# The 64-byte phase of the weight slots that TensorE loads for 256 moving columns: (3, 0) in place of (1, 1)

## The chip, the cores and the metric

One core of one Trainium2 chip. The metric is the device time of one execution in microseconds (us); durations of single instructions are in nanoseconds (ns).

## The reference

Two transformer blocks run one after the other on 256 tokens of width 2048, in float32. The first mixes a state-space branch (SSD) and an attention over selected keys, the second is a softmax attention with forget gates ("Fox"). Each is followed by an MLP with a squared ReLU and 8192 hidden units. Cut to what is large:

```python
def hybrid_layer(x, ...):
    h = rmsnorm(x, g_mix) @ w_in                      # one wide input projection, split into parts
    ...                                               # convolution, SSD, attention
    x = x + concat([y_ssd, y_att]) @ w_out
    u = rmsnorm(x, g_mlp) @ w_up
    return x + square(relu(u)) @ w_down

def second_block(x, ...):
    h = fox_attention(rmsnorm(x, g0), w_in, b_f, w_out)
    x = x + rmsnorm(h, g1)
    h = square(relu(rmsnorm(x, g2) @ w1)) @ w2
    return x + rmsnorm(h, g3)
```

## The kernel before

Each float32 operand is split into a high part (rounded to the type fp32r) and a low part (the rest), and a product is made of three: high by high, high by low and low by high.

The weights stream through a ring of four slots. A slot holds 128 partitions x 2048 values (1024 KB in all). The queue of SyncE brings a chunk into `raw`; ScalarE (ACT) copies it to `wh`, which rounds it (L671); VectorE (DVE) writes raw minus wh to `wl` (L1208), and wl lies in the same memory as raw. TensorE (PE) uses the slot and adds one to `chunk_used`; that lets SyncE refill it. Four slots in a row make a panel of 512 output columns.

Where a slot lies is set by `slot`: its base is a multiple of 256 bytes, and a *phase* moves it by 0 to 3 steps of 64 bytes (`ASIDE` is 16 values of four bytes). Each panel has a pair of phases, one for wh (high) and one for raw and wl (low):

```python
high, low = PHASES.get((b, j), PHASES.get(b, (0, 0)))
at = j * SLOT + ASIDE * (high if buffer is wh else low)
```

The activations (`XHL`, with `XH` and `XL` in it) start on multiples of 256 bytes throughout.

PE takes the panels in four forms:

- *narrow* (`k_tile`, lines 2213 to 2215): the weights are the stationary operand, 128 x 128 at a time, and 256 columns of XH or XL move. For each of the 64 blocks of a panel there are three matmuls: wh by XH, wh by XL, wl by XH, each with a weight load of its own. Eight panels are narrow: the first five of the input projection (`WIN`), the first panel of each MLP (`B_M1`, `B_M2`) and the first of the Fox projection (`B_FOX`). A panel has four slots of 48 such matmuls. Their phases are (1, 1).
- *wide* (`half_cols`, lines 2200 and 2202): wh by 512 columns (XH and XL together), then wl by the 256 of XH. These are the other panels of the MLPs' first products, with phases (1, 0) in the first half of an MLP, behind a first slot ("lead") with (1, 3), and (3, 0) in the second half behind a lead with (3, 2); and seven panels of the Fox projection with (3, 0).
- *rows* (lines 2173 to 2175) and the MLPs' second products (lines 2319 to 2321): the weights are the moving operand, with phases (0, 0).

The order of all this on PE is written out by hand. Between slots PE also does side work by two tables (`MIX_AT`, `FOX_AT`), such as transposes and the small products of the attention. In the opening and at the start of the second MLP it turns pieces of the activations every few matmuls.

Of the kernel before, what the change touches and what calls it, by code (L numbers as in the profile page):

```python
# [73 lines left out]
def hybrid_then_fox(nc, x, g_mix, w_in, conv_w, conv_b, dt_bias, a_log, d_skip, g_ssd, g_q, g_k,  # L74
# [3 lines left out]
    with ctx:  # L78
# [232 lines left out]
        def fox_acc(n):  # L311
# [6 lines left out]
        narrow_chunks = ({B_WIN + n for n, (kind, _) in enumerate(WIN) if kind in TFORM}  # L318
                         | {B_FOX, B_M1, B_M2})
# [1 line left out]
                       | {b0 + half * B_HALF + n for b0 in (B_M1, B_M2) for half in range(2) for n in range(UP)}  # L321
                       - narrow_chunks)

        PHASES = {b: (1, 1) for b in narrow_chunks}
        PHASES.update((b, (3, 0)) for b in wide_chunks)
        for b0 in (B_M1, B_M2):
            for half in range(2):
                first = b0 + half * B_HALF + (half == 0)
                lead, rest = ((3, 2), (3, 0)) if half else ((1, 3), (1, 0))
                PHASES.update((b, rest) for b in wide_chunks if first <= b < first + UP)  # L330
                PHASES[first, 0] = lead

        def slot(buffer, b, j):


            high, low = PHASES.get((b, j), PHASES.get(b, (0, 0)))
            at = j * SLOT + ASIDE * (high if buffer is wh else low)
# [2343 lines left out]
```

How the kernel before makes its waits and increments, by code:

```python
        def wait_full(eng, name):  # L449
            b, n = uses[name]
            eng.wait_ge(side_full[b], n + 1)
# [1 line left out]
        def wait_emptied(eng, name):  # L453
            b, n = uses[name]
            eng.wait_ge(side_free[b], n + 1)
# [1 line left out]
        def wait_free(eng, name):  # L458
            b, n = uses[name]
            if n:
                eng.wait_ge(side_free[b], n)
# [1 line left out]
        def full(ins, name):  # L463
            ins.then_inc(side_full[uses[name][0]], 1)
# [18 lines left out]
            def chunk(w, b, j, k0, col):  # L483
                if not (isinstance(b, int) and b == 0):
                    sp.wait_ge(chunk_used, 4 * b + j - 3)
                src = w[k0 * P:(k0 + 4) * P, col].rearrange("(k p) n -> p k n", p=P)
                sp.dma_start(slot(raw, b, j), src).then_inc(raw_landed[j], 16)
# [5 lines left out]
            def half_panels(w, b, col, kept={}):  # L494
                for j in range(4):
                    sp.wait_ge(chunk_used, 4 * b + j - 3)
                    c, r = col + 256 * (j // 2), 8 * P * (j % 2)
                    sp.dma_start(slot(raw, b, j).rearrange("p a (c n) -> p (a c) n", n=256),
                                 w[r:r + 8 * P, c:c + 256].rearrange("(k p) n -> p k n", p=P))\
                      .then_inc(raw_landed[j], 16)
                    if j in kept:
                        at = (slice(0, P), kept[j] // 2, slice(1024 * (kept[j] % 2), 1024 * (kept[j] % 2) + 1024))
                        sp.wait_ge(sum_ready, 12)
                        sp.dma_start(kept_x[at], X[at]).then_inc(x_kept, 16)
```

## Time and profile before

| | us |
|---|---|
| median of 3 runs | 2182.21 (2181.88 to 2183.65) |
| span of the profiled execution | 2179.8 |
| PE busy | 2162.5 |
| DVE busy | 1437.6 |
| ACT busy | 1026.6 |

The page gives no time of the profiled execution other than its span, which runs from the first instruction to the last. PE's matmuls overlap: one starts while the one before it still drains, so the sum of their durations is larger than the busy time, and the distance between two starts tells how fast they go. In the rows below, PE is TensorE's matmuls, and the rows name an instruction by its line in the kernel and by output and inputs.

### The profile page before, as it was taken

To read this page: it belongs to the slowest core of one execution; us is meant where nothing else is said; L and a number is where in the kernel's file an instruction comes from. 1 tells how busy PE (TensorE), PEld (TensorE's weight loads), DVE (VectorE), ACT (ScalarE), POOL (GpSimd) and SP (SyncE) were. 2 spreads that over 40 slices of the span, in tenths; PEclk is the share of its full clock that TensorE was granted. 3 is DMA by queue.
4 is the path that set the end of the run, shared out by engine and by line. 5 is a ranking of instruction groups with operands and counts; after the bars stand their busy time and mean duration, and the time that the engine had idled before them with its cause. 6 is when DMAs were issued, how large, how long until landed. Compare 5 with 4: busy or idle time off the path is not lost.

```text
span 2179.8 us, 27888 instructions
## 1 busy us (share of the span) xinstructions
PE 2162.5 (99%) x11744; PEld 1867.4 (86%) x11744; DVE 1437.6 (66%) x1748; ACT 1026.6 (47%) x1176; POOL 26.3 (1%) x71
## 2 busy tenths in 40 slices
PE   9999999999999999999999999999999999999998
PEld 9988788988888888888898888889888888888886
DVE  6688664566666766687756654546666766667787
ACT  6453563444443444445444444545444444445453
POOL 1000000000000000000001010000000000000000
PEclk9999999999999999999999999999999999999999
DMA  8455445566666666666566665556666666666665
GB/s 263 144 171 166 153 135 193 174 193 194 193 195 196 203 195 194 193 196 200 186 196 203 189 190 172 174 193 196 206 193 193 197 194 200 194 194 192 204 217 188
DMA packets 256413, 415.49 MB, mean 191 GB/s; under 512 B 13284, under 2 KB 167056, under 8 KB 256032
## 3 DMA queue, kind: packets, MB, share of 16 engines
q1 hardware_dynamic: 254800, 409.89, 59.9%
q0 software_dynamic: 1456, 3.81, 0.6%
q8 instruction: 93, 1.52, 0.3%
q14 instruction: 32, 0.26, 0.0%
q10 hardware_dynamic: 32, 0.01, 0.0%
HBM read 409.47 MB, written 4.21 MB: 190 GB/s over the span
## 4 chain that ended last, share of the span: by engine, by line
PE 96%; DVE 3%; ACT 0%; issue 0%; POOL 0%; DVEq 0%; POOLq 0%; ACTq 0%
PE bank L2200 25%; PE bank L2202 12%; PE bank L2320 10%; PE bank L2321 10%; PE bank L2319 10%; PE bank L2173 5%; PE bank L2175 5%; PE bank L2174 5%; PE bank L2213 3%; PE bank L2215 3%; PE bank L2214 3%; DVE wl L1208 1%; PE bank L2436 1%; PE bank L2261 1%; PE bank L2457 0%; PE bank L2466 0%
## 5 line engine op out<-in xcount | busy, mean ns | idle before, releaser
L1208 DVE TENSOR_TENSOR wl<-raw,wh 128x2048 fp32r<-128x2048 f32 x376 | 860.1, 2290 | 355.0 <-ACT wh L671 353.7
L671 ACT ACTIVATE wh<-raw 128x2048 fp32r<-128x2048 f32 x376 | 721.0, 1919 | 466.4 <-DVE raw L1458 138.4
L2200 PE MATMUL bank<-XHL,wh 128*128 128x512 f32 x2368 | 810.1, 390 | 0.0
L2202 PE MATMUL bank<-XHL,wl 128*128 128x256 f32 x2368 | 654.2, 276 | 0.0
L2200 PEld LDWEIGHTS bank<-XHL,wh 128*128 128x128 f32 x2368 | 444.5, 188 | 93.3 <-issue 0.2
L2202 PEld LDWEIGHTS bank<-XHL,wl 128*128 128x128 f32 x2368 | 444.5, 188 | 0.3
L2319 PE MATMUL bank<-wh,hh 128*128 128x512 f32 x844 | 328.6, 389 | 0.0
L2320 PE MATMUL bank<-wl,hh 128*128 128x512 f32 x844 | 328.4, 389 | 0.0
L2321 PE MATMUL bank<-wh,hl 128*128 128x512 f32 x844 | 328.3, 389 | 0.0
L2173 PE MATMUL bank<-wh,XHL 128*128 128x512 f32 x576 | 229.4, 398 | 0.7 <-DVE XHL L1216 0.7
L2175 PE MATMUL bank<-wh,XHL 128*128 128x512 f32 x576 | 224.7, 390 | 0.0
L2174 PE MATMUL bank<-wl,XHL 128*128 128x512 f32 x576 | 224.2, 389 | 0.0
L797 ACT ACTIVATE RB<-bank 128x256 f32<-128x256 f32 x120 | 39.6, 382 | 345.4 <-PE bank L2202 345.4
L2319 PEld LDWEIGHTS bank<-wh,hh 128*128 128x128 f32 x844 | 158.4, 188 | 33.1
L2320 PEld LDWEIGHTS bank<-wl,hh 128*128 128x128 f32 x844 | 158.4, 188 | 32.9
L2321 PEld LDWEIGHTS bank<-wh,hl 128*128 128x128 f32 x844 | 158.4, 188 | 32.5
L1378 DVE TENSOR_TENSOR RB<-bank,RB 128x256 f32<-128x256 f32 x120 | 45.3, 419 | 198.2 <-ACT RB L797 198.2
L2213 PE MATMUL bank<-XHL,wh 128*128 128x256 f32 x512 | 145.7, 284 | 3.0 <-DVE XHL L1242 1.2
L2214 PE MATMUL bank<-XHL,wh 128*128 128x256 f32 x512 | 142.7, 279 | 0.0
L2215 PE MATMUL bank<-XHL,wl 128*128 128x256 f32 x512 | 142.7, 279 | 0.0
L2175 PEld LDWEIGHTS bank<-wh,XHL 128*128 128x128 f32 x576 | 108.1, 188 | 23.3
L2173 PEld LDWEIGHTS bank<-wh,XHL 128*128 128x128 f32 x576 | 108.2, 188 | 22.8 <-DVE XHL L1216 1.0
(445 smaller groups left out, 1832.7 us busy)
## 6 DMA issues: line engine op xcount, KB each, us to landing
raw<-in_mlp_w_dram SPq DMA_DIRECT2D x128, 1024.0 KB, 5.5
raw<-in_w_up_dram SPq DMA_DIRECT2D x64, 1024.0 KB, 5.4
raw<-in_w_down_dram SPq DMA_DIRECT2D x64, 1024.0 KB, 5.5
raw<-in_fox_w_in_dram SPq DMA_DIRECT2D x48, 1024.0 KB, 5.3
raw<-in_w_in_dram SPq DMA_DIRECT2D x40, 1024.0 KB, 5.0
raw<-in_w_out_dram SPq DMA_DIRECT2D x16, 1024.0 KB, 5.0
raw<-in_fox_w_out_dram SPq DMA_DIRECT2D x16, 1024.0 KB, 5.0
raw<-in_w_in_dram SPq DMA_DIRECT2D x16, 256.0 KB, 8.3
```

The source lines that it names most:

```text
L671: act.activation(slot(wh, b, j), slot(raw, b, j), ACT.Copy).then_inc(hi_ready, 1)
L1208: dve.tensor_tensor(slot(wl, b, j), slot(raw, b, j), slot(wh, b, j).bitcast(F32), ALU.subtract)\
L2173: pe.matmul(o, sh, mh, start=first and kk == 0, stop=False)
L2174: pe.matmul(o, sh, ml, start=False, stop=False)
L2175: mm = pe.matmul(o, sl, mh, start=False, stop=last and kk == 3)
L2200: pe.matmul(bk[:, :].rearrange("p (s t) -> p s t", s=2), sh, XHL[:, k, :, :], start=k == 0, stop=False, skip_group_check=True)
L2202: mm = pe.matmul(bk[:, 0:TOK], sl, XH[:, k, :], start=False, stop=k == KT - 1, skip_group_check=True)
L2213: pe.matmul(o, sh, mh, start=first and f % 2 == 0, stop=False, skip_group_check=True)
L2214: pe.matmul(o, sh, ml, start=False, stop=False, skip_group_check=True)
L2319: pe.matmul(bk[:, :], a[0], w[0], start=first, stop=False)
L2320: pe.matmul(bk[:, :], a[0], w[1], start=False, stop=False)
L2321: return pe.matmul(bk[:, :], a[1], w[0], start=False, stop=last)
```

## The change

The pair of phases of the eight narrow panels becomes (3, 0): wh lies 192 bytes beyond a multiple of 256 instead of 64, raw and wl lie on it instead of 64 beyond. All other panels keep theirs. No instruction is added or taken away.

```diff
-        PHASES = {b: (1, 1) for b in narrow_chunks}
+        PHASES = {b: (3, 0) for b in narrow_chunks}
         PHASES.update((b, (3, 0)) for b in wide_chunks)
         for b0 in (B_M1, B_M2):
             for half in range(2):
```

## Rows read from the trace of the kernel before

**Rows 1.** The page's head and its busy time of PE.
```profile
span 2179.8 us, 27888 instructions
...
PE 2162.5 (99%) x11744; PEld 1867.4 (86%) x11744; DVE 1437.6 (66%) x1748; ACT 1026.6 (47%) x1176; POOL 26.3 (1%) x71
```
**Rows 2.** The page's chain that ended last, by engine.
```profile
PE 96%; DVE 3%; ACT 0%; issue 0%; POOL 0%; DVEq 0%; POOLq 0%; ACTq 0%
```
**Rows 3.** The page's costliest groups: count, busy us, mean ns of one.
```profile
L1208 DVE TENSOR_TENSOR wl<-raw,wh 128x2048 fp32r<-128x2048 f32 x376 | 860.1, 2290 | 355.0 <-ACT wh L671 353.7
L671 ACT ACTIVATE wh<-raw 128x2048 fp32r<-128x2048 f32 x376 | 721.0, 1919 | 466.4 <-DVE raw L1458 138.4
...
L2213 PE MATMUL bank<-XHL,wh 128*128 128x256 f32 x512 | 145.7, 284 | 3.0 <-DVE XHL L1242 1.2
L2214 PE MATMUL bank<-XHL,wh 128*128 128x256 f32 x512 | 142.7, 279 | 0.0
```
**Rows 4.** Timeline of PE, second panel's first slot: start us, duration us.
```profile
33.52 0.28 PE L2213 MATMUL bank<-XHL,wh 128*128 128x256 f32 x1
...
39.18 0.26 PE L2517 MATMUL bank<-ident,PR 110*128 110x110 f32 x1
```
**Rows 5.** Timeline of PE, third panel's first slot.
```profile
61.70 0.28 PE L2213 MATMUL bank<-XHL,wh 128*128 128x256 f32 x1
...
67.15 0.33 PE L2507 MATMUL bank<-ident,SMT 96*128 96x96 f32 x2
```
**Rows 6.** Windows, L2214 alone: length, busy (count), granted clock, DMA share, GB/s.
```profile
21.52:27.95 6.43, 4.46 (x16) 1.00 0.79 291
...
33.61:39.25 5.64, 4.50 (x16) 1.00 0.82 175
...
61.79:67.22 5.43, 4.42 (x16) 1.00 0.01 2
...
101.13:106.77 5.64, 4.49 (x16) 1.00 0.54 183
...
419.83:425.27 5.44, 4.42 (x16) 1.00 0.63 193
...
1499.70:1505.34 5.64, 4.50 (x16) 1.00 0.71 222
```
**Rows 7.** Windows, L2202 alone: lead slot and next slot of both MLPs.
```profile
426.44:430.67 4.23, 3.40 (x12) 1.00 0.82 247
431.72:435.80 4.08, 3.31 (x12) 1.00 0.82 255
1506.50:1510.73 4.23, 3.40 (x12) 1.00 0.88 227
1511.79:1515.86 4.07, 3.31 (x12) 1.00 0.79 244
```
**Rows 8.** Windows, L2202 alone: two runs of the Fox projection, phases (3, 0).
```profile
1211.78:1216.54 4.76, 3.87 (x14) 1.00 0.67 216
1217.58:1222.47 4.89, 3.92 (x14) 1.00 0.71 214
```
**Rows 9.** Groups by line, 34 to 56 us: the copies of narrow slots.
```profile
L1208 DVE TENSOR_TENSOR wl<-raw,wh 128x2048 fp32r<-128x2048 f32 x5 | 11.4, 2288 | 7.9 <-ACT wh L671 7.9
L671 ACT ACTIVATE wh<-raw 128x2048 fp32r<-128x2048 f32 x5 | 9.5, 1909 | 5.9 <-DMA raw<-in_w_in_dram 5.9
```
**Rows 10.** The page's DMA issues: count, size, median us to landing.
```profile
raw<-in_w_in_dram SPq DMA_DIRECT2D x40, 1024.0 KB, 5.0
```
**Rows 11.** Waits of PE, 395 to 430 us: total, times, longest us.
```profile
PE bank L2213 <- DVE wl L1208: 0.5, 1, 0.5
```
**Rows 12.** The chain that ended last, 412 to 420 us: start us, us.
```profile
412.64 0.45 PE bank L2261 x4
...
417.37 2.16 DVE wl L1208
```
**Rows 13.** Waits of DVE, 138 to 150 us.
```profile
DVE U L1323 <- PE bank L2215: 2.7, 1, 2.7
```

## The prediction

> **What bounds the kernel now.** I read the page's head first: the span is 2179.8 us and PE is busy for 99% of it [rows 1]. The profile gives no time of its own for the execution beyond the span; the median of the three runs, 2182.2 us, lies 2.4 us above it, so I carry each difference of the span over to the median one for one. The chain that ended last is PE for 96% [rows 2]. So the question is how fast TensorE issues the matmuls that the edit touches, and whether somebody else makes it wait there.
>
> Those matmuls are lines 2213 to 2215: 512 of each, 1536 in all, each with 256 moving columns and a 128 x 128 weight load of its own from a slot of wh or wl [rows 3]. They make 32 slots of 48 matmuls (eight panels of four). The durations in the page overlap and are no price; the price is the distance between starts. I took two slots that nothing interrupts, and read the timeline of PE. The first slot of the second panel starts at 33.52 us and the next instruction after its 48 matmuls starts at 39.18: 5.66 us, 118 ns each [rows 4]. The first slot of the third panel goes from 61.70 to 67.15: 5.45 us, 113.5 ns each [rows 5]. Both have phases (1, 1), the same shapes and the same granted clock. So with the phases of today the stream goes at one of two paces, and a slot at the long pace costs 0.21 us more than one at the short.
>
> To count the paces I cut one window from the first to the last L2214 of each of the 32 slots. The reader is to divide the busy time by its count: 4.50/16 is 281 ns, 4.42/16 is 276 ns, and the window is 5.64 us long in the first case and 5.43 to 5.46 in the second [rows 6]. The window from 33.61 stands for 14 at the long pace, those from 61.79 and 419.83 for 12 at the short. Six slots are broken by transposes every few matmuls: two of the opening keep the short pace (4.43), and four, for which 21.52 stands, show 4.46, half and half (that one in the opening, three in the second MLP). That is 14 + 2 = 16 slots' worth at the long pace and 16 at the short. The stream keeps its pace until something interrupts PE, and the pace is not tied to what the DMA does at the time (its share is 0.82 and 0.54 in two long windows, 0.01 and 0.63 in two short ones).
>
> **What the phases have to do with it.** Lines 2200 and 2202 have the same kind of stream (512 and 256 moving columns) with other phases. In the first half of each MLP the first wide slot has phases (1, 3), the next ones (1, 0). Over 12 pairs the first takes 4.23 us and the second 4.08, in both MLPs [rows 7]; PE isn't interrupted between them, so the pace changes where the phases do. Twelve starts span 11 distances, so the long pace costs 0.15/11 = 13.6 ns per pair of 768 columns, the same rate as in the narrow slots (0.21 us over 16 x 768 columns is 13 ns). Before this lead slot the narrow slots of the two MLPs ended at different paces (short at 419.83, long at 1499.70 [rows 6]), and both leads go at the long pace and both panels behind them at the short. So the lead forgets what came in.
>
> The Trainium skill ("TensorE: Matmul & The Clock Gate", section "Step-by-step: what each phase is for") says that the moving operand and the weight load have independent read ports, and that loading the next weights takes nothing from the running matmul; by that an address phase is worth nothing and the sum is 2182.2. This trace disagrees, by the 0.15 us per 12 pairs.
>
> **The change, part by part.** It removes, adds and reorders no instruction and no wait. It moves the slots of eight panels by 64-byte steps: wh from 1 to 3, and raw and wl from 1 to 0.
>
> *The copies.* ACT's L671 and DVE's L1208 write at the new phase. In panels with (1, 1) they take 1909 and 2288 ns [rows 9], over the whole kernel, all phases together, 1919 and 2290 [rows 3]. I take nothing; 10 ns either way on 32 copies would be 0.3 us, off PE's path. The cover is the ring of four slots: from the release of a slot to its next use PE has three other slots, 3 x 5.45 = 16.3 us, and the refill needs 5.0 us for the transfer [rows 10] and 1.9 + 2.3 for the copies, 9.2 us. Without that cover each slot would wait.
>
> *The transfers.* raw lands on a multiple of 256 bytes in place of 64 beyond it. The 1024 KB transfers for the narrow panels are among those with a median of 5.0 us [rows 10]; 7 us of slack cover any change.
>
> *The matmuls.* No row has (3, 0) with 256 moving columns each time, so the price is bounded. Below: all 32 slots at the short pace, 16 x 0.21 = 3.4 us saved, plus the two lead slots (16 pairs x 13.6 ns = 0.2 us each) if these take it too: 3.8 us. No steady stretch of the trace goes at a shorter one, so that is the end. Above: all 32 at the long pace, 3.4 us lost. The nearest row is the Fox projection, wide panels with just (3, 0), broken by transposes into 19 runs. Sixteen take 340 ns per pair (the window from 1211.78 stands for them), three go longer, as the one from 1217.58: 4.89 us against 4.76 over 14 pairs, so 0.13/13 = 10 ns per pair [rows 8]. I take that frequency: 3/19 of 32 is 5 slots, at 16 x 10 ns = 0.16 us each, 0.8 us left of the present 3.4.
>
> *What of it arrives.* Behind the first five panels DVE takes over the path: L1323 starts when PE's L2215 ends and DVE had waited 2.7 us for it [rows 13], so an earlier end moves DVE too. In the first MLP PE waits once, 0.5 us, for wl [rows 11]; the chain into that copy starts at PE's own transposes at 412.64 us, ahead of the third slot [rows 12], so two slots' gain passes on and the third slot's 0.2 us is eaten by a longer wait.
>
> Sum: -3.4 + 0.8 + 0.2 = -2.4 us, 2179.8 us.
>
> **The rivals.** (a) *Nothing moves*: the pace is drawn afresh at each interruption and the phase has no say in a 256-column stream, so about half the slots are long again. For it: one and the same phase gives both paces [rows 4, 5]. Against: the switch at the lead slot, and 3 in 19 under (3, 0) against half under (1, 1). 2182.2, with 0.7 either way. (b) *The narrow slots all turn long*: a triple loads high, high, low while the wide pair loads high, low, and (1, 3) shows that some phases always give the long pace. All 32 long: 2182.2 + 3.4 = 2185.6. It decides in the uninterrupted panels: once the second panel or the start of the Fox panel is long, it stays so. (c) *The wide panels inherit it*, the rival on the other side. The lead (1, 3) is followed by 27 slots of (1, 0), 432 pairs, uninterrupted, in each first half. If the new narrow panel hands the lead a pace from which (1, 0) doesn't get to the short one, these cost 432 x 10 to 13.6 ns = 4.3 to 5.9 us per MLP: with the gain above, 2184.1 for one MLP to 2191.6 for both at the dear price. It decides at the first pairs of (1, 0): 353 ns per pair there instead of 340. Against it stands that both incoming paces ended alike. (d) *A pace shorter than any shown*: 5 ns less in each of 1536 matmuls would save another 7.7 us, 2179.8 - 7.7 = 2172 us; no row has it.
>
> **How the numbers follow.** More slots short (2178.4 to 2181.4): 0.50. Nothing moves (2181.4 to 2183): 0.20. Narrow slots long (2183 to 2185.6): 0.16. Wide panels inherit: 0.10. A shorter pace: 0.04. The forecast is 2179.8. A measurement tells about 0.2%, 4.4 us, from no change, so the bounds are 2177.8 and 2186.6. Below: the 0.04, and 0.04 for the lower edge of the first case with the runs' own spread of 1.8 us. Above: 0.09 of the inherited case and 0.02 of the long one. Within: 0.81. The range of 8 in 10 is 2178.0 to 2186.5; the likeliest case alone has 2178.4 to 2181.4.
>
> **What would show it.** Windows of L2214 per slot: mostly 276 ns and 5.43 to 5.46 us, five or so above, and the unbroken panels from 33.6, 401 and 1092 us at the short pace. The pairs behind the two leads at 340 ns; if they stand at 350 or more, (c) holds. Copies of L671 and L1208 within 10 ns, and PE's wait for wl near 419 us longer by 0.2. It is wrong if half the L2214 windows are still 5.64 us long (a), if nearly all are (b), or if windows are shorter than 5.43 (d).

## The result

The changed kernel takes 2185.43 us in the median of 17 runs (2185.06 to 2186.82), the kernel before 2182.21 (17 runs): 3.2 us more, a ratio of 1.0015 with a 95% interval of 1.0008 to 1.0022. It is inside the 0.2% that the prediction allowed a measurement to tell, but on the other side of no change from the forecast of 2179.8.

The head of the page after, its chain, and the narrow groups:

```profile
span 2184.6 us, 27888 instructions
...
PE 2167.3 (99%) x11744; PEld 1873.4 (86%) x11744; DVE 1437.8 (66%) x1748; ACT 1027.0 (47%) x1176; POOL 28.5 (1%) x71
...
PE 96%; DVE 3%; ACT 0%; issue 0%; POOL 0%; DVEq 0%; POOLq 0%; ACTq 0%
...
L2213 PE MATMUL bank<-XHL,wh 128*128 128x256 f32 x512 | 146.8, 287 | 2.9 <-DVE XHL L1242 1.2
...
L2214 PE MATMUL bank<-XHL,wh 128*128 128x256 f32 x512 | 144.4, 282 | 0.0
```

DVE and ACT do what they did [rows 1]; PE is busy 4.8 us longer, and L2214's mean has gone from 279 ns [rows 3] to 282. Where that comes from is seen in the windows from the first to the last L2214 of a slot, for the slots of [rows 6]:

```profile
21.93:28.46 6.53, 4.49 (x16) 1.00 0.74 276
...
34.12:39.77 5.65, 4.50 (x16) 1.00 0.86 191
...
62.30:67.94 5.64, 4.49 (x16) 1.00 0.01 2
...
102.84:108.49 5.65, 4.49 (x16) 1.00 0.55 183
...
422.36:428.00 5.64, 4.49 (x16) 1.00 0.62 186
...
1504.49:1510.12 5.63, 4.48 (x16) 1.00 0.66 211
```

In these rows the third number is the length of the window in us and the fourth the busy time of its 16 matmuls. The slots at 62 and 422 us were 5.43 and 5.44 long and are now 5.64; those that were long have stayed so. All 26 slots that nothing breaks up every few matmuls show 5.63 to 5.65. So none is left at the short pace: the 16 slots' worth that had it lost 16 x 0.21 = 3.4 us, against a measured 3.2. In the order of time, the last window of the input projection ends at 144.00 instead of 141.49, that of the first MLP's narrow panel at 428.00 instead of 425.27, that of Fox at 1118.97 instead of 1116.02: the delay grows only where narrow panels run.

The wide panels don't take part. These windows on L2202 hold 12 pairs of the lead slot and of the next, in the first MLP and in the second, as [rows 7]:

```profile
429.18:433.41 4.23, 3.40 (x12) 1.00 0.78 247
434.47:438.54 4.07, 3.31 (x12) 1.00 0.80 257
1511.28:1515.51 4.23, 3.39 (x12) 1.00 0.92 234
1516.56:1520.64 4.08, 3.31 (x12) 1.00 0.81 249
```

The spans differ by 4.8 us, the medians by 3.2. The rest is a dip of TensorE's granted clock at the start of the second MLP, which this execution has and the profiled one of the kernel before has not. The windows of PE there, the first three of the changed kernel and the last two of the kernel before (behind the busy times of the five engines stand the granted clock, the DMA share and the GB/s):

```profile
1480.00:1483.00 3.00, 1.52 (x12) 1.04 (x10) 1.90 (x4) 1.45 (x5) 0.00 (x0) 1.00 1.04 378
1483.00:1487.00 4.00, 3.84 (x20) 3.84 (x21) 3.78 (x6) 3.92 (x3) 0.00 (x0) 0.59 0.14 50
1487.00:1491.00 4.00, 4.00 (x36) 4.00 (x36) 2.31 (x6) 2.73 (x5) 0.00 (x0) 0.99 0.00 2
```

```profile
1477.00:1480.00 3.00, 1.56 (x13) 1.08 (x11) 1.89 (x5) 1.41 (x5) 0.00 (x0) 1.00 1.03 378
1480.00:1484.00 4.00, 3.80 (x33) 3.80 (x34) 3.79 (x6) 4.00 (x4) 0.00 (x0) 1.00 0.18 65
```

In the changed kernel PE was busy for 1.52 of 3 us, and in the next 4 us the granted clock was 0.59 (mostly the level of 1.2 GHz): 20 matmuls fall into them, where the 4 us behind hold 36. In the kernel before PE was busy for 1.56 of 3 us, and the clock stayed at 1.00. The dip isn't the change's: the unchanged kernel, profiled once more further down, has it too (a granted clock of 0.57 from 1481 to 1485 us). The 17 times of the changed kernel lie in two groups, eleven up to 2185.66 us with the median among them, and six from 2186.32 with the profiled execution among them.

### The profile page after: what moved, and what is told of

The parts are those of the page before. It is cut to its first block, busy times and chain, and to the rows that moved or that the text cites. A ratio compares the mean times of both kernels' runs of the same rounds, so it can differ in the third digit from the quotient of the medians.

```text
span 2184.6 us, 27888 instructions
## 1 busy us (share of the span) xinstructions
PE 2167.3 (99%) x11744; PEld 1873.4 (86%) x11744; DVE 1437.8 (66%) x1748; ACT 1027.0 (47%) x1176; POOL 28.5 (1%) x71
## 3 DMA queue, kind: packets, MB, share of 16 engines
q8 instruction: 93, 1.52, 0.3%
## 4 chain that ended last, share of the span: by engine, by line
PE 96%; DVE 3%; ACT 0%; issue 0%; POOL 0%; DVEq 0%; POOLq 0%; ACTq 0%
PE bank L2200 25%; PE bank L2202 12%; PE bank L2319 10%; PE bank L2321 10%; PE bank L2320 10%; PE bank L2173 5%; PE bank L2175 5%; PE bank L2174 5%; PE bank L2213 3%; PE bank L2214 3%; PE bank L2215 3%; DVE wl L1208 1%; PE bank L2436 1%; PE bank L2261 1%; PE bank L2457 0%; PE bank L2466 0%
## 5 line engine op out<-in xcount | busy, mean ns | idle before, releaser
L1208 DVE TENSOR_TENSOR wl<-raw,wh 128x2048 fp32r<-128x2048 f32 x376 | 860.3, 2290 | 355.7 <-ACT wh L671 354.1
L671 ACT ACTIVATE wh<-raw 128x2048 fp32r<-128x2048 f32 x376 | 721.1, 1919 | 467.5 <-DVE raw L1458 137.8
L2202 PE MATMUL bank<-XHL,wl 128*128 128x256 f32 x2368 | 654.2, 276 | 0.0
L2202 PEld LDWEIGHTS bank<-XHL,wl 128*128 128x128 f32 x2368 | 444.6, 188 | 0.3
L2319 PE MATMUL bank<-wh,hh 128*128 128x512 f32 x844 | 328.6, 389 | 0.0
L2319 PEld LDWEIGHTS bank<-wh,hh 128*128 128x128 f32 x844 | 158.4, 188 | 32.6
L2214 PE MATMUL bank<-XHL,wh 128*128 128x256 f32 x512 | 144.4, 282 | 0.0
```

Source lines behind the costliest of these rows:

```text
L671: act.activation(slot(wh, b, j), slot(raw, b, j), ACT.Copy).then_inc(hi_ready, 1)
L1208: dve.tensor_tensor(slot(wl, b, j), slot(raw, b, j), slot(wh, b, j).bitcast(F32), ALU.subtract)\
L2202: mm = pe.matmul(bk[:, 0:TOK], sl, XH[:, k, :], start=False, stop=k == KT - 1, skip_group_check=True)
L2319: pe.matmul(bk[:, :], a[0], w[0], start=first, stop=False)
```

## The experiments

A window from the first L2214 of a slot to the last holds 15 triples (wh by XH, wh by XL, wl by XH), one duration of 0.28 us and 0.06 us of margin. So 5.44 is 340 ns per triple, 5.54 is 347, 5.59 is 350, 5.64 is 353, 5.68 is 356, 5.74 is 360. A window with twelve of the wide L2202 holds 11 pairs: 4.07 is 340 ns per pair, 4.19 is 350, 4.23 is 353. Measured times stand beside runs of the kernel before on the same chip.

**Half of the change each, and two equal pairs.** The edit is the one pair of line 324.

```diff
-        PHASES = {b: (1, 1) for b in narrow_chunks}
+        PHASES = {b: (3, 1) for b in narrow_chunks}    # n31; n10: (1, 0); n33: (3, 3); n00: (0, 0)
```

> Narrow panels with phases (3, 1): the high half of the change alone. Theory H (wh at phase 3 is what forces the long pace of 118 ns): nearly all 32 slots long, 2185.4 us, +3.2. Theory L (wl at phase 0 forces it): the slots stay mixed or turn short, 2179 to 2182.2 us. Theory U (any pair of unequal phases forces it): all long, 2185.4 us.

> Narrow panels with phases (1, 0): the low half of the change alone. Theory H (wh at phase 3): mixed or short, 2179 to 2182.2 us. Theory L (wl at phase 0): nearly all slots long, 2185.4 us. Theory U (unequal phases): all long, 2185.4 us.

> Narrow panels with phases (3, 3). Theory H (wh at phase 3): all slots long, 2185.4 us. Theory L (wl at phase 0): mixed or short, 2179 to 2182.2 us. Theory U (unequal phases): mixed or short, 2179 to 2182.2 us.

> Narrow panels with phases (0, 0). Theory H (wh at phase 3): mixed or short, 2179 to 2182.2 us. Theory L (wl at phase 0): all slots long, 2185.4 us. Theory U (unequal phases): mixed or short, 2179 to 2182.2 us.

| phases | us | before, us | ratio (95%) |
|---|---|---|---|
| (3, 1) | 2182.55 | 2182.79 | 1.0000 (0.9990 to 1.0009) |
| (1, 0) | 2185.99 | 2182.79 | 1.0013 (1.0004 to 1.0023) |
| (3, 3) | 2183.70 | 2182.79 | 1.0004 (0.9995 to 1.0014) |
| (0, 0) | 2188.78 | 2182.79 | 1.0028 (1.0019 to 1.0038) |

The windows of L2214, two with (3, 1):

```profile
402.20:407.64 5.44, 4.42 (x16) 1.00 0.64 193
...
420.36:426.05 5.69, 4.53 (x16) 1.00 0.58 184
```

one with (1, 0):

```profile
403.84:409.48 5.64, 4.51 (x16) 1.00 0.60 186
```

one with (0, 0):

```profile
405.92:411.66 5.74, 4.53 (x16) 1.00 0.61 183
```

The high half of the change is harmless: with (3, 1), 15 of the 26 slots that aren't broken up are short, and the long ones are a little longer (357 ns). (3, 3) has 9 short ones. The low half does all of the damage: (1, 0) has no short slot, and neither has (0, 0). (One slot of (1, 0), the last of the Fox panel, went at 365 ns.) Theory H falls by (3, 1), and theory U by (0, 0), where the phases are equal. Theory L stands, but it didn't foresee that (0, 0) is longer still: 5.74 instead of 5.64 for 32 slots is another 3.2 us.

**All other pairs.** Each kernel has different pairs in three or four groups of panels.

```diff
+        PHASES = {b: (2, 2) if b < B_WIN + 2 else (1, 3) if b < B_M1 else (2, 1) for b in narrow_chunks}   # scan1
```

> Three pairs of phases in one kernel: (2, 2) in the first two panels of the input projection, (1, 3) in its next three, (2, 1) in the first panels of the MLPs and of the Fox projection. Read is the distance of three matmuls (a triple), 340 ns short and 353 or more long. Theory P (an even low phase rules the short pace out, an odd one allows it): (2, 2) has 353 or more in all 8 slots; (1, 3) and (2, 1) have some slots at 340. Theory Z (only the low phase 0 does it): (2, 2) has some slots at 340 too.

> Three pairs in one kernel: (1, 2) in the first two panels, (3, 2) in the next three, (0, 1) in the other three. Theory P (an even low phase rules the short pace out): no slot at 340 in the first 20, some in the last 12. Theory Z (only the low phase 0 does it): some slots at 340 in each of the three parts.

> Half steps, 32 bytes: (0.5, 0.5) in the first two panels, (1.5, 1.5) in the next three, (2.5, 2.5) in the other three. If whole lines of 64 bytes set the pace, each does as the whole phase below it: 360 ns per triple with 0.5, mixed 340 and 353 with 1.5, and with 2.5 as with (2, 2). If the distance of the two streams counts to finer steps, one of them may keep 340 in all its slots.

> The four pairs not yet seen: (2, 3) in the first two panels, (0, 3) in the next three, (2, 0) in the first panels of the first MLP and of Fox, (0, 2) in that of the second MLP. Theory O (the short pace is open only where both phases are odd): no slot at 340 ns per triple. Theory L (only the low phase decides): (2, 3) and (0, 3) have slots at 340.

Windows of L2214, the first kernel, (2, 2), then (1, 3), then (2, 1):

```profile
34.86:40.54 5.68, 4.51 (x16) 1.00 0.92 214
...
63.20:68.64 5.44, 4.42 (x16) 1.00 0.01 3
...
402.35:408.03 5.68, 4.50 (x16) 1.00 0.60 185
```

The second, (3, 2), then (0, 1):

```profile
74.53:80.07 5.54, 4.43 (x16) 1.00 0.57 189
...
403.32:408.97 5.65, 4.50 (x16) 1.00 0.62 186
```

The fourth, (2, 3) twice, then (0, 3):

```profile
33.95:39.54 5.59, 4.43 (x16) 1.00 0.82 168
...
51.18:56.93 5.75, 4.51 (x16) 1.00 0.57 182
62.49:68.14 5.65, 4.53 (x16) 1.00 0.01 2
```

The whole times of these four kernels (one run each: 2185.19, 2184.30, 2187.94 and 2186.83 us) mix their panels and decide nothing. Read in this way, ns per triple (where two stand, both occur in the slots that nothing breaks up):

| high \ low | 0 | 1 | 2 | 3 |
|---|---|---|---|---|
| 0 | 360 | 353 | 357 | 353 |
| 1 | 353, 365 | **340**, 353 | 355 | **340** |
| 2 | 355 | 353 to 356 | 356 | 350, 360 |
| 3 | 353 | **340**, 357 | 347, 353 | **340**, 353 |

The short pace occurs in four of the sixteen pairs, those with both phases odd, and (1, 3) had it in all 12 slots. So it isn't the low phase 0 (theory Z), nor the low phase alone (P and L: (2, 1) and (0, 3) have an odd low phase and no short slot), but any even phase on either side; O, formed on these, held in the fourth kernel.

How firmly a field says "no short pace" depends on where its pair was tried, for (1, 1) isn't short everywhere either. (0, 0), (1, 0) and (3, 0) stood in all eight panels. (3, 2) and (0, 3) stood in the last three panels of the input projection, where the kernel before has 10 of 12 slots short. But (1, 2), (2, 2) and (2, 3) stood in the first two panels, where the kernel before has none of five unbroken slots short, and (0, 1), (2, 1), and by turns (2, 0) and (0, 2), in the last three, where it has two of nine. Of (0, 2) there is one unbroken slot. For these the rule is likely rather than shown; only (2, 3) was seen in all panels, in a kernel further down.

Half steps bring no short pace: (0.5, 0.5) took 355 ns, (1.5, 1.5) 352 to 360 and (2.5, 2.5) 360. They don't go as the whole phase below them either (360, then 340 and 353, then 356), so the expectation that whole steps of 64 bytes set the pace failed.

**Relative to what?** The first try moved XHL by 64 bytes.

```diff
-        arena = region(arena, [("XHL", [P, KT, 2, TOK], F32R)])
+        arena = region(arena + 64, [("XHL", [P, KT, 2, TOK], F32R)])    # x64; x64p also moves the phases
-            return -(-at // LINE) * LINE
+            return -(-(at - 64) // LINE) * LINE + 64                     # all64, without the line above
```

> Narrow phases (1, 1) as before; the moving operand XHL lies 64 bytes further on. Theory R (what counts is the weights' phase relative to the moving operand's): the narrow slots do as (0, 0) did, 360 ns per triple in all 32. Theory A (the weights' own address counts): 340 and 353 mixed, as before. The other panels' relative phases move too, so the whole time says nothing here.

> XHL 64 bytes further on, and each phase of the narrow and wide panels one step on from a pair seen at 340: narrow (2, 0), which is (1, 3) moved with XHL; wide (2, 0) and (2, 1), then (0, 3) and (0, 1). Theory R (what counts is the weights' phase relative to the moving operand's): narrow slots at 340 per triple, wide panels at 340 per pair. Theory A (the weights' own address counts): even phases, so narrow at 353 or more, wide as in the kernel that moved XHL alone, 353.

> Every tensor that matmuls read, the slots and XHL alike, lies 64 bytes further on; phases (1, 1) as before. Theory R (weights relative to the moving operand): nothing changes, 340 and 353 mixed in the narrow slots, 2182 us. Theory A (the address itself; (1, 1) now does as (2, 2) and the wide (1, 0) as (2, 1)): no narrow slot at 340, wide panels long, 2185 us and more.

Both expectations of the first two kernels rested on a slip of mine: wh begins where XHL ends, so it moved along, and only raw and wl stayed. Relative to XHL, the narrow slots at (1, 1) were at (1, 0) then, not at (0, 0), and in the second kernel at (2, 3), not at (1, 3). Windows of L2214 with XHL (and wh) moved:

```profile
405.41:411.05 5.64, 4.50 (x16) 1.00 0.61 186
```

and with the phases moved too:

```profile
34.43:40.17 5.74, 4.51 (x16) 1.00 0.86 199
40.30:45.89 5.59, 4.43 (x16) 1.00 0.72 239
```

The first has what (1, 0) had, 353 ns in all 26 unbroken slots and no short one, the second mostly the mix of 350 and 360 that (2, 3) had, and in all panels no slot at 340. The clean test is the kernel that moves everything. Its narrow windows (L2214), and the lead and the next slot (L2202):

```profile
34.15:39.79 5.64, 4.50 (x16) 1.00 0.87 208
...
62.33:67.76 5.43, 4.42 (x16) 1.00 0.01 2
```

```profile
427.58:431.81 4.23, 3.40 (x12) 1.00 0.78 246
432.86:436.93 4.07, 3.31 (x12) 1.00 0.81 257
```

Short and long are mixed as at (1, 1), 10 of the 26 short. In the first two panels, the only ones where (2, 2) was tried, the unbroken slots stand at the 5.64 of (1, 1) and not at the 5.68 of (2, 2). The wide panels have their 4.23 and 4.07 as before. The time is 2183.43 against 2182.33 us, a ratio of 1.0004 (0.9995 to 1.0014). So the phase counts relative to the moving operand (R), and the address itself doesn't (A).

**Is the mix at (1, 1) chance?** The kernel before, unchanged.

> The kernel before once more, one look. If the pace of a narrow slot at (1, 1) is drawn by chance at each interruption, other slots are long than in the first profile, and about half of them; if it follows from the order of the work, the same 14 slots and the same four halves are long.

It took 2183.54 us in its one run. The same 14 slots are long but for one (the last of the second MLP's panel); among the six that are broken up three differ. So most of the mix recurs. But it doesn't follow from the order of the work alone. The kernel with (1, 1) and no leads, further down, is the kernel before up to 424 us, and there five of the slots that nothing breaks up differ: three of the second panel are short, the last of the third and the last of the first MLP's panel long. Windows of L2214 in it, one short and one long:

```profile
40.10:45.54 5.44, 4.42 (x16) 1.00 0.73 241
...
420.06:425.70 5.64, 4.50 (x16) 1.00 0.60 186
```

The slot at 40 us turned behind a transpose between two slots, where the profile shows no wait of PE. So at (1, 1) an interruption can change the pace, and which way it goes isn't settled by the program; what settles it stays open. The counts of short slots above (15, 9, 10) are each of one execution.

**The pair that is always short, in all eight panels.**

```diff
-        PHASES = {b: (1, 1) for b in narrow_chunks}
+        PHASES = {b: (1, 3) for b in narrow_chunks}
```

> All eight narrow panels with (1, 3), the pair whose 12 slots all went at 340 ns per triple. Theory O (the short pace is open only where both phases are odd, and (1, 3) always takes it): 32 slots at 340, 16 x 0.21 = 3.4 us less than before, 2178.8 us. Rival (the first panels after other work enter another way than those in the middle of the input projection): the panels of the MLPs and of Fox stay at 353, about 2181 us. If the lead slot keeps 353 per pair, nothing is given back behind it.

2179.22 us against 2182.39, a ratio of 0.9986 (0.9977 to 0.9995). Windows of L2214 and PE's wait between 395 and 435 us:

```profile
33.46:38.89 5.43, 4.42 (x16) 1.00 0.83 164
...
399.97:405.42 5.45, 4.42 (x16) 1.00 0.63 192
...
1497.41:1502.85 5.44, 4.42 (x16) 1.00 0.76 236
```

```profile
PE bank L2213 <- DVE wl L1208: 0.7, 1, 0.7
```

All 26 slots that aren't broken up show 5.43 to 5.48. The gain is 3.2 us: the 3.4 us that the prediction's lower bound gives the narrow slots, less the 0.2 us by which PE waits longer for wl than the 0.5 of [rows 11]. This kernel is faster than the one before and so than the changed one. The other expectation, that panels behind other work stay at 353, failed; and the leads kept 353 per pair, so they don't take the short pace that comes in.

**The leads.** Does the wide panel take over the pace of the narrow one?

```diff
-                PHASES[first, 0] = lead
+                if half:
+                    PHASES[first, 0] = lead    # nolead30: narrow (3, 0); nolead13: (1, 3); nolead11: (1, 1)
```

> The changed kernel without the lead slot (1, 3) in the first half of each MLP: (3, 0) in the narrow panel, then (1, 0) at once. If the lead is what keeps the wide panels from inheriting the narrow panel's pace, all 7 panels of both MLPs go at 350 to 353 ns per pair, 448 pairs x 10 to 13 ns = 4.5 to 6 us each: 2194 to 2197 us. If (1, 0) finds its pace by itself: 340 per pair and two leads less at 0.2 us each, 2185.0 us.

> The kernel before, (1, 1) narrow, without the lead slot of the first halves, one look. Before, the first MLP's narrow panel ends short and the second's long. Theory I (the wide panels inherit the pace that comes in): the first MLP's wide panels at 340 per pair, the second's at 350 or more, about +4.5 us in all if the narrow slots keep their mix. Rival (without the lead, (1, 0) goes long whatever comes in): both at 350 or more, +9 us.

> The (1, 3) kernel without the lead slot of the first halves. Theory I (the wide panels inherit the incoming pace, here 340): 340 per pair from the first pair on and no lead to pay, 0.4 us less than with it, 2178.8 us. Rival ((1, 0) goes long whatever comes in): 350 per pair in 2 x 448 pairs, 9 us more less 0.4, 2188 us.

With (3, 0) and no lead the kernel takes 2194.57 us against 2182.39, a ratio of 1.0052 (1.0037 to 1.0068): 12.2 us more instead of 3.2, so the lead is worth 9 us to the changed kernel. With (1, 1) it is 2190.52 (one run, before 2182.33): in that run both narrow panels ended long, so it tells nothing of a short pace coming in. With (1, 3), where it comes in short, it is 2189.39, a ratio of 1.0028 (1.0015 to 1.0041). Four of its five runs took 2189.28 to 2190.90 us, the fifth 2183.55. Windows of L2202 in the first and second wide slot, with (3, 0) (L2203 in that kernel):

```profile
429.41:433.60 4.19, 3.37 (x12) 1.00 0.81 249
434.66:438.85 4.19, 3.37 (x12) 1.00 0.82 250
```

and with (1, 3), both MLPs:

```profile
424.98:429.05 4.07, 3.31 (x12) 1.00 0.82 258
430.25:434.47 4.22, 3.37 (x12) 1.00 0.79 248
1511.52:1515.59 4.07, 3.31 (x12) 1.00 0.87 222
1516.79:1520.98 4.19, 3.37 (x12) 1.00 0.81 254
```

Theory I is right for the first slot, which keeps the 340 that came in. It loses it at the second. The timeline of PE there in the first MLP, and of DVE:

```profile
428.87 0.39 PE L2200 MATMUL bank<-XHL,wh 128*128 128x512 f32 x1
429.09 0.28 PE L2202 MATMUL bank<-XHL,wl 128*128 128x256 f32 x1
429.24 0.50 PE L2200 MATMUL bank<-XHL,wh 128*128 128x512 f32 x1
429.58 0.28 PE L2202 MATMUL bank<-XHL,wl 128*128 128x256 f32 x1
```

```profile
426.90 2.29 DVE L1208 TENSOR_TENSOR wl<-raw,wh 128x2048 fp32r<-128x2048 f32 x1 [1.01 <-ACT wh L671]
```

DVE ends the low part at 429.19, PE's next slot starts at 429.24 instead of 429.20, and from the first pair on the panel goes at 350 to 353 ns, for seven panels. In the second MLP the same slot starts as late. So (1, 0) keeps the pace that comes in, short or long, and after this start went long both times; behind the lead (1, 3) it goes at 340. That 0.04 us of waiting is what turned it is shown by the place alone and wasn't tried by itself. The fifth run fits a first MLP that kept the short pace: 432 pairs at 353.4 instead of 340 ns make 5.8 us, and it is 5.8 us below the median. That is an estimate, since no trace of that run was kept.

## Why the prediction was wrong

*What bounds the kernel, and the two paces*: right. PE's chain has the same 96%, and the count of 16 long and 16 short slots carries every sum here: 16 x 0.21 = 3.4 us stands for 3.2 lost with (3, 0) and 3.2 gained with (1, 3).

*The matmuls*: this is the step that failed: "I take that frequency: 3/19 of 32 is 5 slots". It took the share of (3, 0) in the Fox panels, where a pair has 512 and 256 moving columns, for that of a stream with 256 each time. In the narrow stream (3, 0) has no short pace at all: 0 of 32 slots instead of 27. So the term isn't 0.8 us but 32 x 0.21 = 6.7. The bounds of +3.4 and -3.4 us set around it held for this change, which went to the upper one, and the kernel with (1, 3) went to the lower; but "all at the long pace" isn't the end for every pair, since (0, 0) has a longer one and costs 6.0 us. That a pair's pace doesn't carry over is seen both ways: (1, 3), long in both leads, is short in all narrow slots. It couldn't be read from the trace before, which has no pair of phases in both streams, so the share was a guess.

*The rivals*: (b) came true, with its time (2185.6 against 2185.43) and at the place that it named. Its ground, that (1, 3) always gives the long pace, is a reading from the wide stream too and is wrong for the narrow one, so that (b) came true is in part luck. And that the measured time lies inside the stated range is no merit of the forecast: the range reaches 4.3 us above no change and so takes in (b). (a) is excluded by the slots that were short and are long now. (c) did not come: both panels behind the leads stand at 340. "So the lead forgets what came in" is right, and the runs without a lead show what hung on it: 9 us. (d) has no row in any run; 340 ns is the floor of all of them.

*The copies, the transfers*: right. L671 and L1208 take 1908 and 2289 ns between 34 and 56 us, as in [rows 9], and PE waits for wl for the same 0.5 us:

```profile
PE bank L2213 <- DVE wl L1208: 0.5, 1, 0.5
```

*What of it arrives*: the term of 0.2 us that a longer wait would eat didn't apply to a slower panel, and it showed in the quicker one (0.7 against 0.5).

*The rule on the independent read ports* (the Trainium skill, "TensorE: Matmul & The Clock Gate", section "Step-by-step: what each phase is for"): these runs disagree with it, and by more than the lead did: 340 and 360 ns per triple of 768 columns, 20 ns against 13.6. Kernels that differ in nothing but the phase of the loaded weights, (1, 3) and (0, 0), are 3.2 us below and 6.0 us above the kernel before, 9.2 us apart in 1536 matmuls. Why the phase of the loaded weights against the moving operand sets the pace, why an even one left no short pace and an odd pair may go either way, and why (1, 0) has no short pace with 256 columns but has one with 512 and 256, stays open: no run here looks below the distance of two starts.

## What to carry to other kernels

A distance between starts that differs between two stretches of the same matmuls is worth looking for, since the page's means hide it: count the stretches at each pace first, for that bounds what a change of layout can give or cost. Don't carry the share of one kind of stream over to another; sixteen pairs could be tried in a handful of kernels, since each panel of one kernel can have its own. But then each pair is seen in its own place only, and the place has a say in the pace, so try the best pair in all places, as was done here with (1, 3). And a pace that is lost when something stops PE, as with (1, 0) in the wide panels, needs something that restores it, as the lead slot does here.

## What the runs showed that was not expected

The phase of the moving weights matters too. With wh moved by 64 bytes against hh and hl, the MLPs' second products, whose weights are the moving operand, got longer. Windows that hold 24 of the matmuls of L2319, in the kernel before and in the kernel that moved XHL and wh:

```profile
579.08:595.17 16.09, 9.34 (x24) 1.00 0.62 194
```

```profile
589.22:605.78 16.56, 9.53 (x24) 1.00 0.59 188
```

In the kernel that moved everything it is 16.09 again. Together with the wide panels, which went from 340 to 353 ns per pair, this made the kernel that moved XHL and wh take 2235.85 us (one run, the kernel before 2182.74), 53 us for 64 bytes; with the phases moved too it took 2235.64. How the 53 us divide between these products, the wide panels and the rest was not tried.
